# RWKV's inverse levels: both halves' products first, then both halves' transposes, in TensorE's order

## The reference, cut to what matters

```python
def step(S, inp):
    r_t, w_t, k_t, v_t, kk_t, a_t = inp
    sa = jnp.einsum("bhvk,bhk->bhv", S, kk_t)
    S = (S * w_t[:, :, None, :]
         - sa[..., None] * (kk_t * a_t)[:, :, None, :]
         + v_t[..., None] * k_t[:, :, None, :])
    return S, jnp.einsum("bhvk,bhk->bhv", S, r_t)
```

## Time and profile before

| | |
|---|---|
| median of 3 runs | 4413.92 us (4412.43 to 4415.04) |
| the profiled execution | 4413.05 us, span 4411.3 us |
| TensorE matmuls busy | 4136.8 us, 94% of the span |
| VectorE, ScalarE busy | 2412.4 us (55%), 1622.1 us (37%) |
| levels 0 to 2, first `level_z` to the next level 3 | 151.93 us for the 8 pairs |
| levels 3 and 4, up to `y_products` | 128.96 us for the 8 pairs |

### The profile page before, as it was taken

One profiled execution on the slowest core, in us unless ns is written; L12 is line 12 of the kernel. 1 busy time (PEld: TensorE's weight loads), 2 busy tenths in 40 slices (PEclk: granted clock), 3 DMA queues, 4 the chain that ended last, 5 costly groups with the idle time before them and its releaser, 6 DMA issues. The chain is left out here.

```text
span 4411.3 us, 90967 instructions
## 1 busy us (share of the span) xinstructions
PE 4136.8 (94%) x40018; PEld 3519.7 (80%) x40018; DVE 2412.4 (55%) x3777; ACT 1622.1 (37%) x2881; POOL 154.3 (3%) x131
## 2 busy tenths in 40 slices
PE   6999999999899999799998988999989999888998
PEld 4667666667667777699998668999989999657998
DVE  3445555455323333376665455665676565556777
ACT  3333333333223444353333334433343333334443
POOL 0000000000000000000000030000000000020000
PEclk9999999999899999899999999999999999999999
DMA  4000000001534444211121111112111212111232
GB/s 159 18 18 23 23 22 17 18 14 41 220 148 156 170 158 149 96 67 67 68 76 71 39 46 48 67 67 77 68 48 68 77 67 72 67 55 58 101 111 77
DMA packets 74730, 332.18 MB, mean 75 GB/s; under 512 B 4577, under 2 KB 41826, under 8 KB 46050
## 3 DMA queue, kind: packets, MB, share of 16 engines
q1 hardware_dynamic: 74338, 326.37, 20.7%
HBM read 324.26 MB, written 2.10 MB: 74 GB/s over the span
## 5 line engine op out<-in xcount | busy, mean ns | idle before, releaser
L845 PE MATMUL banks<-x_hi,w_hi 128*128 128x384 f32 (+1 forms) x2496 | 807.7, 324 | 26.2 <-DVE x_lo L1119 22.2
L846 PE MATMUL banks<-x_lo,w_hi 128*128 128x384 f32 (+1 forms) x2496 | 805.2, 323 | 0.0
L847 PE MATMUL banks<-x_hi,w_lo 128*128 128x384 f32 (+1 forms) x2496 | 804.8, 322 | 0.0
L931 ACT CAST w_hi<-landing_all 128x512 fp32r<-128x512 f32 x768 | 457.3, 619 | 327.9 <-DVE landing_all L1030 300.1
L1022 DVE TENSOR_TENSOR w_lo<-landing_all,w_hi 128x512 fp32r<-128x512 f32 x768 | 516.8, 685 | 50.5 <-ACT w_hi L931 50.0
L845 PEld LDWEIGHTS banks<-x_hi,w_hi 128*128 128x128 f32 x2496 | 473.8, 190 | 30.6 <-DVE x_lo L1119 23.4
L846 PEld LDWEIGHTS banks<-x_lo,w_hi 128*128 128x128 f32 x2496 | 473.9, 190 | 0.4
L847 PEld LDWEIGHTS banks<-x_hi,w_lo 128*128 128x128 f32 x2496 | 473.7, 190 | 0.0
L845 PE MATMUL banks<-g_hi,w_hi 128*128 128x384 f32 (+1 forms) x1232 | 421.3, 342 | 0.0
L846 PE MATMUL banks<-g_lo,w_hi 128*128 128x384 f32 (+1 forms) x1232 | 421.3, 342 | 0.0
L847 PE MATMUL banks<-g_hi,w_lo 128*128 128x384 f32 (+1 forms) x1232 | 421.2, 342 | 0.0
(11 more groups left out here) (438 smaller groups left out, 6663.0 us busy)
## 6 DMA issues: line engine op xcount, KB each, us to landing
landing_all<-in_w SPq DMA_DIRECT2D x132, 1024.0 KB, 4.8
arena_first<-in_ada_w SPq DMA_DIRECT2D x44, 2048.0 KB, 8.4
weight_ring_first<-in_rw_pair SPq DMA_DIRECT2D x32, 512.0 KB, 4.2
weight_ring_first<-in_da_head SPq DMA_DIRECT2D x8, 2048.0 KB, 12.6
landing_all<-in_w_in SPq DMA_DIRECT2D x12, 1024.0 KB, 4.9
weight_ring_first<-in_ada_w SPq DMA_DIRECT2D x4, 2048.0 KB, 10.8
landing_all<-in_w_out SPq DMA_DIRECT2D x8, 1024.0 KB, 4.9
x_res<-in_x_t SPq DMA_DIRECT2D x2, 2048.0 KB, 12.9
```

Source lines behind the costliest of these rows:

```text
L845: mm(o, wh, xh, start=first, stop=False, skip_group_check=onto)
L846: mm(o, wh, xl, start=False, stop=False, skip_group_check=onto)
L847: return mm(o, wl, xh, start=False, stop=last, skip_group_check=onto)
L931: nc.scalar.copy(SH[:, q % RING], raw(q)).then_inc(whi.h, 1)
```

## The change

In each level the loop over the two halves is cut in two at two places. Before, TensorE took products and transposes of half 0, then products and transposes of half 1, then the second products and the fourth kind of half 0, then those of half 1. Now both halves' products come first, then both halves' transposes, then both second products, then both halves' fourth kind. The waits stand before the same instructions as ahead of the change. No other engine's code is changed.

```diff
@@ -1599,6 +1599,7 @@
                                 pe.wait_ge(as_ready.h, as_ready.at(i, e + 1))
                             pe.wait_ge(x_ready.h, x_ready.at(i, 2 * l + e + 1))
                             level_z(i, e)
+                        for e in range(2):
                             if 1 <= l <= 3:
                                 pe.wait_ge(tm_ready.h, tm_ready.at(i, 2 * (l - 1) + e + 1))
                             if l == 4:
```

## The result

The changed kernel takes 4439.93 us (median of 4 runs, 4431.51 to 4447.98), the kernel before 4413.4 us (4 runs, 4412.43 to 4415.04): ratio 1.0062, 95% interval 1.005 to 1.0074. It is slower by 26.5 us, where I had forecast no difference and a range up to 4421.

What follows compares the result with a forecast made beforehand. The levels were taken to run at the pace of instruction packets, 256 instructions in about 3.72 us. Levels 0 to 2 +0.5, level 3 0, level 4 -1.3: -0.8 us on 4413.05, forecast 4413, own range 4407 to 4419, wider 4404 to 4421.

Steps and rivals of the forecast that it cites:

- What bounds the levels: Levels: TensorE's instructions arrive in packets of 256, each taking its work or about 3.72 us, whichever is longer.
- Work removed: Levels 0 to 2: four of eight tile-size changes go, 0.66 us; with the added wait 5.68 us a level for 6.03.
- The wait added: Before half 0's second products TensorE waits 0.34 us for ScalarE's copy, 1.78 us after the transposes instead of 1.44.
- Hence a pace: Levels: 256 instructions take their work or about 3.72 us, whichever is longer; a longer packet gives nothing to the next.
- The walk through five packets: Levels 0 to 2: packet times summed over five packets, 19.32 us before and 19.38 after, 6.37 and 6.39 a level.
- +0.5 us for levels 0 to 2: Levels 0 to 2 of all pairs: 24 x 0.02 us slower, from packet times of 6.39 us a level for 6.37.
- -1.3 us for the last two levels: Level 3 unchanged; level 4 keeps half of its 0.32 us of saved work, 8 x 0.16 us.
- Rival B: Levels: two in five packets, not one, hold both slow transpose zones, 4.50 us each; slower, 4423; chance 0.08.
- Rival C: Levels: ScalarE's copy of half 0 starts only after all twelve transposes, wait 0.64 us longer; slower, 4427; chance 0.04.
- Rival A: Levels: packets don't hold TensorE back, its work sets the time; gain 11.0 us, 4403, up to 4390; chance 0.11.

Runs made afterwards that it cites:

- before_twice: The kernel before with half 0's first products issued twice in each level: 4461.32 us, ratio 1.0123 to the kernel before.
- after_joined: The changed kernel with mask's and copy's signals of a half on one semaphore, so second products wait once: 4410.63 us, ratio 0.9997 to the kernel before.
- after_swapped: The changed kernel with the two waits ahead of the second products in the other order: 4406.38 us, ratio 1.0001 to the kernel before.

## Why the prediction was wrong, point by point

- *What bounds the levels:* right. The pace of the packets does; `before_twice` shows it, 53.8 us where work alone would give 27.6.
- *Work removed, 0.35 us a level:* right. Where neither border nor late request disturbs a level it takes 5.69 us in `after_joined` and `after_swapped`, for 5.68 predicted; the kernel before has 6.0 there. Little of it comes through, for those two kernels are as fast as before (0.9997 and 1.0001), as the forecast of no difference had it.
- *The wait added:* its size was right, 1.83 us from transposes to second products for 1.78; the step from the copy's end to the second products, for which I took 0.06 us, measured 0.11. The failing step is the sentence on what stands behind it: I named "everything of the level, and VectorE for it" as queued behind the waiting TensorE, and left out the one thing that I had just found, the request for instructions. With it went the step "Hence a pace: 256 instructions take their work or about 3.72 us, whichever is longer": I took the time from border to request as fixed, one microsecond. It isn't while the sequencer stands in a separate wait. The sequencer ran ahead of the engine: `after_swapped` passed the same place at 273.9, before the first of the twelve transposes (24 instructions) went at 274.12. So in the changed kernel it can stand there from soon after the border at 275.12 to 277.1, though TensorE idles only 0.54; the start of the standing is no row, and is my estimate from these two kernels. After a border 31 to 79 instructions ahead of the wait the next request takes 3.1 to 3.9 us, the packet 5.7 to 6.1. The walk through five packets had no such packet: 3.72 and 4.50 us were its two sizes. Its +0.5 us for levels 0 to 2 measured +15.6, and the -1.3 us for the last two levels +11.6.
- The kernel before held a hint. Where 2 to 62 instructions lay between a border and half 0's separate wait, 12 levels, the packet moved 1.0 to 1.5 us after that wait was passed, up to 1.7 us after the border; and TensorE's weight loads idled only 0.17 us ahead of half 0's second products, the same in all 40 levels. So what the packet followed, the end of the separate wait, didn't show as idle time of the engine there.
- *Rival B* had the sign and a third of the size (4423), by a mechanism that fell. Packets of over 4.4 us, by which I would have known it, did come, but from late requests. *Rival C* fell at once: the copy starts 0.92 us after the first transpose (276.30 after 275.38). *Rival A* fell with the pace. The clock had no share in the forecast: the ten late requests left stops of 0.5 to 2.1 us, and 1.2 and 0.9 us after the ends of two of them (2.09 us at 401.78, 1.92 at 545.39) the granted clock fell to 0.50 for 3.4 us.

The copy's row for that, ScalarE in level 2 of pair 1:

```profile
276.30 1.50 ACT L1748 COPY x_res<-banks 128x768 f32<-128x768 f32 x2 [2.71 <-PE banks L1499]
```

What stays open: why the danger ends between 79 and 81 instructions, with one exception at 64; why the changed kernel's runs spread over 16 us; and whether a carried wait would stop the sequencer too if it lasted longer than here.

## What to carry to other kernels

Where TensorE works on small tiles, count its instructions as a resource: divide them by 256 and look whether the work of one packet takes longer than the pace that the trace shows. Here that mattered only in stretches of small tiles: behind 2000 us, where 256 instructions of wide products (L845 to L847) take some 21 us, a packet starts to move a median of 2.6 us ahead of a border in the kernel before and 2.4 in the changed one, and TensorE idles at most 0.05 us at any of the borders there. Where two waits stand ahead of one instruction, write them so that the one which comes late is carried by the instruction, or join them on one semaphore: in the changed kernel that alone was worth 0.6%, in the kernel before nothing that can be told. And before adding a wait ask what the sequencer, not the engine, has to do meanwhile.

## What the runs showed of the hardware

- Instructions for TensorE arrived in 317 packets of 16 KB, 256 instructions each. In the levels the packet starts to move mostly 1.1 us after the border and moves for 0.9 to 1.4 us; where TensorE has stopped, it goes on 1.2 to 1.6 us after the packet's end. Between two borders with a stop at each lie 3.45 to 4.02 us in the levels of the kernel before.
- Where the separate wait of half 0 lay 2 to 79 instructions behind a border, the packet moved 1.0 to 1.7 us after the end of the wait, in 39 of 40 levels of three kernels: at 278.3 for a wait passed at 277.1; at the same border with the late wait carried, 275.1.
- Of the two waits written ahead of the second products, the later written was the separate one: passed 0.04 us after the copy's end in all 40 levels of the changed kernel, before the copy's end in all 40 of `after_swapped`. Exchanging them moved the time from 4439.9 to 4406.4 us (before: 4413.4 and 4407.5 beside them).
- 1.2 us after a stop of 2.09 us in the levels the granted clock fell to 0.50 for 3.4 us, and twelve transposes took 1.87 us of weight loads for 1.29.
